# Delta rule: the 16x16 diagonal blocks inverted on VectorE, one block per partition, instead of in four doubling levels on TensorE

## The chip, the core and the metric

The kernel runs on one core of a Trainium2 chip. The metric is the device time of one execution in microseconds (us), lower being better. In the profile PE is TensorE (PEld its weight loads), DVE is VectorE, ACT is ScalarE, POOL is GpSimd and SP is SyncE, which issues the weight transfers.

## What is computed

Two decoder layers on 256 tokens of width 2048. Each has a mixer and a SwiGLU block, both with a residual and a layer norm. Layer 0's mixer is a gated short convolution beside a gated delta rule of 8 heads x 128; layer 1's is a sparse attention. The change is inside the delta rule:

```python
c = DN_CHUNK                                     # 64
a_mat = where(strict, einsum(kbeta, kc) * decay, 0.0)
rhs = concatenate([vc * bc, kbeta * exp(gc)[..., None]], axis=-1)
sol = triangular_solve(eye(c) + a_mat, rhs, left_side=True, lower=True, unit_diagonal=True)
...
v_new = u_i - w_i @ state
o     = q_i @ state + a_i @ v_new
state = state * gl + k_i.T @ v_new
```

The kernel solves the triangular system by building the inverse of (I + A). It works on chunks of 128 tokens, which gives the same result as the reference's chunks of 64.

## The kernel before

**Matmuls in three passes.** Every weight matrix comes in slabs of 1 MB. A slab is two *halves* of 128x1024. For each half ScalarE writes a rounded copy, `w_hi` (line 599), VectorE writes the rest, `w_lo` (line 1089), and TensorE runs three passes over the pair (lines 1792 to 1794), twelve matmuls of 512 columns. There are four slots for halves: ScalarE may write half h only when TensorE has used half h-4 (`half_used`), and VectorE follows ScalarE. In the program of each engine `halves(n)` (`z_halves(n)` on TensorE) stands where the next n halves are worked on. The order of everything is written out by hand; nothing moves at run time.

**The delta rule stage.** The 256 tokens are two tiles t, the 8 heads two groups hh of four; the four pairs (t, hh) are called *units*. All tiles of a unit are 128x512, four heads side by side. For every unit TensorE fills four PSUM banks (lines 2093 to 2102): `row` and `beta` are per-token numbers spread over all partitions (one matmul of `ones` with a tile that VectorE prepared, lines 1431 and 1432), `kk` and `kq` are products of keys and queries. VectorE makes AT (the transposed A) and the masked E from them (lines 1440 to 1453), with one Exp on ScalarE in between. `by_head` (line 2085) is four matmuls of 128x128, one for each head.

**The levels.** The inverse is built by doubling: given the inverse X of the diagonal blocks of width b (and its transpose T), one level gives that of width 2b. `BLOCKS` has seven levels. Level 0 takes no product: X = I - E on VectorE, then four transposes a unit on TensorE for T (`eT`, line 2105). Each of the levels 1 to 6 is, for each unit, `g` (E by T), a copy to SBUF by ScalarE (line 834), `x` (G by X) and, but for the last, `t` (X by G). VectorE subtracts the results and masks the next E (lines 1470 to 1472).

**Filler.** Between these steps TensorE works on the 16 halves of the next projection (z), `z_halves`: 1 before the units, 2 in each unit, 2 in the `eT` step, and 1 in each of the levels 1 to 5. ScalarE's `z_out` empties the z banks.

**After the stage.** The rest of the delta rule follows, then the output projection. SyncE loads x over the delta rule's tiles, so its queue waits for `gb_free` before it goes on (line 471); the weights behind it in the queue wait too.

Of the kernel before, what the change touches and what calls it, by code (L numbers as in the profile page):

```python
# [21 lines left out]
P = 128  # L22
# [30 lines left out]
BLOCKS = (1, 2, 4, 8, 16, 32, 64)  # L53
# [23 lines left out]
def trunk(nc, x_in, positions, ln_mix_g, ln_mix_b, ln_ffn_g, ln_ffn_b, ffn_w_in, ffn_w_out,  # L77
# [6 lines left out]
    with ctx:  # L84
# [33 lines left out]
        blk_mask = sb("blk_mask", [P, len(BLOCKS), P])  # L118
        lnT = sb("lnT", [P, 2, KT])
# [31 lines left out]
        def dn_tile(n):  # L151
            base, m = (gb_flat, n) if n < 8 else (vT_flat, n - 8)
            return base[:, m * 512:(m + 1) * 512].rearrange("p (h d) -> p h d", h=4)
        dn_more = sb("dn_more", [P, 12, 512], offset=x_at)

        def tiles_of(t, hh):

            if t == 0:
                return [dn_tile(6 * hh + n) for n in range(6)]
            return [dn_more[:, 6 * hh + n, :].rearrange("p (h d) -> p h d", h=4) for n in range(6)]  # L160
# [5 lines left out]
        norm_sq, norm_q = dn_tile(6), dn_tile(7)  # L166
# [78 lines left out]
        ident_ready, out_ready = sem("ident_ready"), sem("out_ready")  # L245
        for_act, for_pe, from_act, gb_free = sem("for_act"), sem("for_pe"), sem("from_act"), sem("gb_free")
# [22 lines left out]
        uses([("eT", t, hh) for t, hh in units])  # L269
# [111 lines left out]
        hands([("rows", t, hh) for t, hh in units])  # L381
        for n in range(len(BLOCKS)):
            hands([("m", t, n, hh) for t, hh in units])
# [120 lines left out]
        def _(pool):  # L504
# [22 lines left out]
            for n, b in enumerate(BLOCKS):  # L527

                v = blk_mask[:, n, :].rearrange("p (m a r) -> p m a r", a=2, r=b)[:, :, 1, :]
                own(pool.memset(v, 1.0))  # L530
                select(v, [[-2 * b, P // (2 * b)], [0, b]], 0, 1, 0.0)
                select(v, [[2 * b, P // (2 * b)], [0, b]], b - 1, -1, 0.0)
            pool.memset(eps_ln[:, :], LN_EPS).then_inc(consts, 1)
# [8 lines left out]
            def layer_norm(n, g, b):  # L542
                pool.wait_ge(gb_free, n + 1)
                if n:
                    pool.wait_ge(x_scaled, NT * n)
                for a, v in enumerate((g, b)):
                    pool.dma_start(gb[:, a, :], bcast(v, D)).then_inc(gb_in, 16)
                pool.dma_start(lnT[:, :, :], ln_by_feature[:, n, :, :]).then_inc(gb_in, 16)
            layer_norm(0, ln_mix_g[0], ln_mix_b[0])
# [36 lines left out]
        def _(act):  # L586
# [265 lines left out]
            for t, hh in units:  # L852
                wait_sp_read(act, ("row", t, hh))
                dt_ = tiles_of(t, hh)[0]
                done(act.activation(dt_, dt_, ACT.Exp))
                halves(2)
            halves(2)
            for n in range(1, len(BLOCKS)):
                for t, hh in units:
                    put(("g", t, n, hh), tiles_of(t, hh)[5])  # L860
                if n < len(BLOCKS) - 1:
                    halves(1)
                if n == 1:
                    z_out(0)
# [190 lines left out]
        def _(dv):  # L1055
# [248 lines left out]
            dv.wait_ge(consts, 3)  # L1304
            halves(LEAD)
# [98 lines left out]
            own(dv.scalar_tensor_tensor(nbe, egc, -1.0, beta, ALU.mult, ALU.mult))  # L1404
            for hh in range(2):
                wait_sp_read(dv, ("ktok", hh))
# [22 lines left out]
            for t, hh in units:  # L1429
                _, _, _, T, _, G = tiles_of(t, hh)  # L1430
                dv.tensor_tensor(G, bc(upper[:, :], 4), over(g_[:, heads_of(t, hh)], P), ALU.mult)
                to_pe(dv.tensor_tensor(T, bc(ident[:, :], 4), over(beta[:, heads_of(t, hh)], P), ALU.mult), ("rows", t, hh))
            halves(1)
            for t, hh in units:
                Dt, AT, E, T, X, G = tiles_of(t, hh)
                name = ("row", t, hh)
                wait_sp(dv, name)
                for h in range(4):
                    n = 8 * t + 4 * hh + h
                    ins = dv.scalar_tensor_tensor(Dt[:, h, :], sp4(name)[:, h, :], ngc[:, n:n + 1], neg_lower[:, :], ALU.add, ALU.add)  # L1440
# [12 lines left out]
                to_pe(dv.tensor_tensor(X, bc(ident[:, :], 4), E, ALU.subtract), ("m", t, 0, hh))  # L1453
                halves(2)

            for t, hh in units:
                Dt, AT, E, T, X, G = tiles_of(t, hh)
                name = ("eT", t, hh)
                wait_sp(dv, name)
                sp_out(dv.tensor_tensor(T, bc(ident[:, :], 4), sp4(name), ALU.subtract), name)  # L1460
                to_pe(dv.tensor_tensor(E, AT, bc(blk_mask[:, 1, :], 4), ALU.mult), ("m", t, 1, hh))
                if hh:
                    halves(1)
            for n in range(1, len(BLOCKS)):
# [12 lines left out]
                if n == 2:  # L1477
                    z_scaled(0)
# [291 lines left out]
        def _(pe):  # L1770
# [320 lines left out]
            def flat(tile):  # L2091
                return tile.rearrange("p h d -> p (h d)")
            for t, hh in units:
                v = slice(t * P, (t + 1) * P)
                _, _, _, T, _, G = tiles_of(t, hh)
# [12 lines left out]
            for n in range(1, len(BLOCKS)):  # L2108
                for t, hh in units:
                    _, _, E, T, X, G = tiles_of(t, hh)  # L2110
                    handed(("m", t, n, hh))
# [310 lines left out]
```

## Time and profile before

| | |
|---|---|
| time, median of 3 runs | 2503.22 us (2503.02 to 2504.13) |
| profiled execution, its own time | 2504.05 us |
| its span | 2502.3 us |
| PE busy | 2427.0 us, 97% |
| DVE busy | 1441.6 us, 58% |
| ACT busy | 1139.3 us, 46% |
| POOL busy | 30.2 us, 1% |
| HBM traffic | 175 GB/s over the span |
| mean granted clock of TensorE | 0.994 |

Busy times say how long an engine had work, not that it held the others up. The chain of waits follows the work that ended last back to its start. Matmul records overlap, so the pace of TensorE is read from the chain or from start to start, not from the mean of one record. An fp32 matmul shows as two records, an fp32 transpose or an fp32r matmul as one.

### The profile page before, as it was taken

To read this page: it belongs to the slowest core of one execution; us is meant where nothing else is said; L and a number is where in the kernel's file an instruction comes from. 1 tells how busy PE (TensorE), PEld (TensorE's weight loads), DVE (VectorE), ACT (ScalarE), POOL (GpSimd) and SP (SyncE) were. 2 spreads that over 40 slices of the span, in tenths; PEclk is the share of its full clock that TensorE was granted. 3 is DMA by queue.
4 is the path that set the end of the run, shared out by engine and by line. 5 is a ranking of instruction groups with operands and counts; after the bars stand their busy time and mean duration, and the time that the engine had idled before them with its cause. 6 is when DMAs were issued, how large, how long until landed. Compare 5 with 4: busy or idle time off the path is not lost.

```text
span 2502.3 us, 33337 instructions
## 1 busy us (share of the span) xinstructions
PE 2427.0 (97%) x12809; PEld 2079.1 (83%) x12809; DVE 1441.6 (58%) x1782; ACT 1139.3 (46%) x1527; POOL 30.2 (1%) x71
## 2 busy tenths in 40 slices
PE   8999999899999999999999998999999999999997
PEld 8999889777888888888879887888788888888886
DVE  5658676566444444455577756766644444445556
ACT  4445633444444444444454545554544444434443
POOL 2000000100000000000000000000000000000000
PEclk9999999999999999999999999999999999999999
DMA  7555431355555555555555653236555555555552
GB/s 254 185 168 185 152 101 51 152 186 168 190 196 177 193 188 196 203 201 197 189 185 159 231 186 101 85 101 219 164 179 195 186 196 188 184 200 214 191 195 107
DMA packets 179448, 437.99 MB, mean 175 GB/s; under 512 B 7104, under 2 KB 19504, under 8 KB 165280
## 3 DMA queue, kind: packets, MB, share of 16 engines
q1 hardware_dynamic: 177632, 427.85, 50.4%
q0 software_dynamic: 1728, 8.92, 0.9%
q8 instruction: 62, 1.02, 0.2%
q14 instruction: 26, 0.21, 0.0%
HBM read 434.64 MB, written 2.10 MB: 175 GB/s over the span
## 4 chain that ended last, share of the span: by engine, by line
PE 91%; DVE 5%; ACT 2%; DMA 1%; issue 1%; SPq 0%; DVEq 0%; ACTq 0%
PE bank L1792 28%; PE bank L1794 28%; PE bank L1793 28%; PE bank L2088 3%; PE bank L2321 1%; DVE w_lo L1089 1%; PE bank L2010 1%; PE bank L2294 1%; DMA raw<-in_hy_w_out_dram 1%; DVE stats L1164 1%; DVE x L1163 1%; DVE yt L1187 0%; ACT w_hi L599 0%; PE bank L2063 0%; PE bank L2312 0%
## 5 line engine op out<-in xcount | busy, mean ns | idle before, releaser
L1089 DVE TENSOR_TENSOR w_lo<-raw,w_hi 128x1024 fp32r<-128x1024 f32 x776 | 943.0, 1224 | 905.5 <-ACT w_hi L599 903.5
L599 ACT ACTIVATE w_hi<-raw 128x1024 fp32r<-128x1024 f32 x776 | 819.6, 1062 | 1072.7 <-PE bank L1794 1052.3
L1792 PE MATMUL bank<-w_hi,xt_hi 128*128 128x512 f32 x1904 | 750.0, 394 | 14.1 <-DVE w_lo L1089 8.3
L1794 PE MATMUL bank<-w_hi,xt_lo 128*128 128x512 f32 x1904 | 743.3, 390 | 0.0
L1793 PE MATMUL bank<-w_lo,xt_hi 128*128 128x512 f32 x1904 | 742.8, 390 | 0.0
L1792 PEld LDWEIGHTS bank<-w_hi,xt_hi 128*128 128x128 f32 x1904 | 358.8, 188 | 89.0 <-issue 10.0
L1794 PEld LDWEIGHTS bank<-w_hi,xt_lo 128*128 128x128 f32 x1904 | 358.5, 188 | 75.6
L1793 PEld LDWEIGHTS bank<-w_lo,xt_hi 128*128 128x128 f32 x1904 | 359.0, 189 | 72.5
L1792 PE MATMUL bank<-xt_hi,w_hi 128*128 128x256 f32 x928 | 267.7, 289 | 12.1 <-DVE w_lo L1089 12.1
L1792 PE MATMUL bank<-w_hi,a_hi 128*128 128x512 f32 x672 | 261.8, 390 | 2.0 <-ACT big L723 1.6
L1794 PE MATMUL bank<-xt_hi,w_lo 128*128 128x256 f32 x928 | 263.7, 284 | 0.0
L1793 PE MATMUL bank<-xt_lo,w_hi 128*128 128x256 f32 x928 | 263.7, 284 | 0.0
L1794 PE MATMUL bank<-w_hi,a_lo 128*128 128x512 f32 x672 | 261.5, 389 | 0.0
L1793 PE MATMUL bank<-w_lo,a_hi 128*128 128x512 f32 x672 | 261.4, 389 | 0.0
L1792 PEld LDWEIGHTS bank<-xt_hi,w_hi 128*128 128x128 f32 x928 | 179.3, 193 | 14.5 <-issue 11.6
L1793 PEld LDWEIGHTS bank<-xt_lo,w_hi 128*128 128x128 f32 x928 | 179.4, 193 | 2.0 <-issue 1.9
L1794 PEld LDWEIGHTS bank<-xt_hi,w_lo 128*128 128x128 f32 x928 | 179.3, 193 | 0.0
L1792 PEld LDWEIGHTS bank<-w_hi,a_hi 128*128 128x128 f32 x672 | 126.1, 188 | 29.4 <-issue 3.2
L1794 PEld LDWEIGHTS bank<-w_hi,a_lo 128*128 128x128 f32 x672 | 126.1, 188 | 26.3
L1793 PEld LDWEIGHTS bank<-w_lo,a_hi 128*128 128x128 f32 x672 | 126.2, 188 | 26.0
L1792 PE MATMUL bank<-spare_hi,xt_hi 128*128 128x512 f32 x80 | 33.1, 413 | 11.7 <-DVE spare_lo L1089 6.9
L714 ACT ACTIVATE yt<-bank 128x512 f32<-128x512 f32 x44 | 24.0, 597 | 43.5 <-PE bank L1794 43.5
(304 smaller groups left out, 1630.3 us busy)
## 6 DMA issues: line engine op xcount, KB each, us to landing
raw<-in_ffn_w_in_dram SPq DMA_DIRECT2D x176, 1024.0 KB, 5.1
raw<-in_ffn_w_out_dram SPq DMA_DIRECT2D x88, 1024.0 KB, 4.8
raw<-in_hy_w_in_dram SPq DMA_DIRECT2D x57, 1024.0 KB, 5.2
raw<-in_nsa_w_in_dram SPq DMA_DIRECT2D x41, 1024.0 KB, 5.1
raw<-in_hy_w_out_dram SPq DMA_DIRECT2D x16, 1024.0 KB, 5.0
raw<-in_nsa_w_out_dram SPq DMA_DIRECT2D x16, 1024.0 KB, 5.1
raw<-in_cmp_w_k_dram SPq DMA_DIRECT2D x4, 1024.0 KB, 6.4
raw<-in_cmp_w_v_dram SPq DMA_DIRECT2D x4, 1024.0 KB, 5.6
```

Of the source, the lines that this page charges most:

```text
L599: act.activation(weights_of(h)[0], half_of(h), ACT.Copy).then_inc(w_hi_ready, 1)
L714: ins = act.activation(sg[:, t, :], b[t][:, :], ACT.Silu)
L1089: dv.tensor_tensor(lo, half_of(h), hi.bitcast(F32), ALU.subtract).then_inc(w_lo_ready, 1)
L1163: own(dv.scalar_tensor_tensor(v, v, ALPHA, acc_bank(n, t, c)[:, :], ALU.mult, ALU.add))
L1164: ins = dv.bn_stats(stats[:, t, c, :], v)
L1792: pe.matmul(dst, l_hi, r_hi, start=start, stop=False, skip_group_check=shared)
L1793: pe.matmul(dst, l_hi, r_lo, start=False, stop=False, skip_group_check=shared)
L1794: return pe.matmul(dst, l_lo, r_hi, start=False, stop=stop, skip_group_check=shared)
L2010: ins = pe.transpose(b[:, f * SEQ + t * P:f * SEQ + (t + 1) * P], hid[:, t, (2 * a + f) * P:(2 * a + f + 1) * P], ident[:, :])
L2088: ins = pe.matmul(b[:, h * P:(h + 1) * P], lhs(h), rhs(h), start=True, stop=True)
L2294: ins = pe.matmul(b[:, h * kn:(h + 1) * kn], qT[:, 4 * g + hp * k + h, v], ksT[:, br, g, 0:kn], start=True, stop=True)
L2321: ins = pe.matmul(b[:, h * P:(h + 1) * P], pT_buf[br][:, k, h * P:(h + 1) * P], vs[:, br, k, g * DH:(g + 1) * DH], start=k == 0, stop=k == t)
```

## The change

A new buffer layout puts each kind of tile of all 16 (tile, head) pairs side by side: `AT_all`, `T_all`, `X_all` and so on. The levels 1, 2, 4 and 8 of `BLOCKS` go, with their masks. In their place VectorE inverts all 128 diagonal 16x16 blocks at once, one block on each partition. Four transposes of 32 partitions x 512 bring the blocks over. For 14 columns j, each a multiply and an add that need the result of the one before, the elimination runs along the free dimension. Eight more transposes write the result into T and X, which GpSimd has set to zero. In the diff the part at line 546 is GpSimd's, that at 853 ScalarE's, those at 1426 and 1450 VectorE's, and that at 2090 TensorE's. `low_half` tells which of the two blocks of a 32x32 square a partition has. TensorE's `row` and `beta` become four matmuls each of a broadcast column with `ident`, so VectorE prepares no tiles for them. The filler z halves are handed out anew: 1, then 1 in each unit, 9 behind the last unit, and 1 in each of the first two levels left.

```diff
-BLOCKS = (1, 2, 4, 8, 16, 32, 64)
+BASE = 16
+BLOCKS = (16, 32, 64)
...
+        dn_more = sb("dn_more", [P, 3, 2048], offset=x_at)
+        def all_heads(v):
+            return v.rearrange("p (m d) -> p m d", m=16)
+        AT_all, T_all = all_heads(gb_flat[:, 0:2048]), all_heads(gb_flat[:, 2048:4096])
+        X_all, Dt_all, E_all, G_all = all_heads(vT_flat), *(all_heads(dn_more[:, n, :]) for n in range(3))
...
+        base_rows = base_flat[:, 0:512].rearrange("p (c r) -> p c r", c=BASE)
+        base_wide = base_flat[:, 512:1024].rearrange("p (i s j) -> p i s j", i=BASE, s=2)
@@ -546,6 +567,12 @@
+            pool.memset(T_all, 0.0).then_inc(base_cleared, 1)
+            wait_sp(pool, ("vtok", NT - 1, 1))
+            pool.memset(X_all, 0.0).then_inc(base_cleared, 1)
@@ -853,15 +880,15 @@
                 done(act.activation(dt_, dt_, ACT.Exp))
-                halves(2)
-            halves(2)
-            for n in range(1, len(BLOCKS)):
+                halves(1)
+            halves(6)
+            z_out(0)
+            halves(3)
+            for n in range(len(BLOCKS)):
@@ -1426,10 +1456,6 @@
-            for t, hh in units:
-                _, _, _, T, _, G = tiles_of(t, hh)
-                dv.tensor_tensor(G, bc(upper[:, :], 4), over(g_[:, heads_of(t, hh)], P), ALU.mult)
-                to_pe(dv.tensor_tensor(T, bc(ident[:, :], 4), over(beta[:, heads_of(t, hh)], P), ALU.mult), ("rows", t, hh))
@@ -1450,18 +1476,43 @@
                 own(dv.tensor_tensor(E, AT, bc(blk_mask[:, 0, :], 4), ALU.mult))
-                to_pe(dv.tensor_tensor(X, bc(ident[:, :], 4), E, ALU.subtract), ("m", t, 0, hh))
-                halves(2)
-
-            for t, hh in units:
-                Dt, AT, E, T, X, G = tiles_of(t, hh)
-                name = ("eT", t, hh)
-                wait_sp(dv, name)
-                sp_out(dv.tensor_tensor(T, bc(ident[:, :], 4), sp4(name), ALU.subtract), name)
-                to_pe(dv.tensor_tensor(E, AT, bc(blk_mask[:, 1, :], 4), ALU.mult), ("m", t, 1, hh))
-                if hh:
-                    halves(1)
-            for n in range(1, len(BLOCKS)):
+                halves(1)
...
+            for rows, cols in quadrants():
+                ins = dv.transpose(base_rows[rows], AT_all[rows, :, cols].rearrange("p m (s c) -> p c s m", s=2))
+            own(ins)
+            halves(1)
+            low, high = low_half[:, 4:5], low_half[:, 5:6]
+            own(dv.scalar_tensor_tensor(base_neg, base_rows[:, :, 0:BASE], low, base_rows[:, :, BASE:], ALU.mult, ALU.add))
+            own(dv.tensor_tensor(base_neg, base_neg, base_below[:, :, :], ALU.mult))
+            own(dv.tensor_tensor(base_inv, base_neg, base_ident[:, :, :], ALU.add))
+            halves(1)
+            for j in range(1, BASE - 1):
+                n = BASE - 1 - j
+                step = base_step[:, 0:n, 0:j]
+                own(dv.tensor_tensor(step, base_neg[:, j + 1:, j:j + 1].to_broadcast([P, n, j]),
+                                     base_inv[:, j:j + 1, 0:j].to_broadcast([P, n, j]), ALU.mult))
+                own(dv.tensor_tensor(base_inv[:, j + 1:, 0:j], base_inv[:, j + 1:, 0:j], step, ALU.add))
+                if j % 4 == 0:
+                    halves(1)
+            halves(1)
+            dv.tensor_scalar(base_wide[:, :, 0, :], base_inv, low, None, ALU.mult)
+            own(dv.tensor_scalar(base_wide[:, :, 1, :], base_inv, high, None, ALU.mult))
+            dv.wait_ge(base_cleared, 2)
+            for rows, cols in quadrants():
+                dv.transpose(T_all[rows, :, cols].rearrange("p m (s j) -> p j s m", s=2), base_wide[rows].rearrange("p i s j -> p j s i"))
+            halves(2)
+            for rows, cols in quadrants():
+                ins = dv.transpose(X_all[rows, :, cols].rearrange("p m (s i) -> p i s m", s=2), base_wide[rows])
+            to_pe(ins, ("base",))
+            halves(1)
+            for n in range(len(BLOCKS)):
@@ -2090,25 +2141,22 @@
-                handed(("rows", t, hh))
-                for name, m in (("row", G), ("beta", T)):
-                    b = sp_use((name, t, hh))
-                    sp_done(pe.matmul(b[:, :], ones[:, :], flat(m), start=True, stop=True), (name, t, hh))
+                m = 8 * t + 4 * hh
+                for name, row in (("row", 4), ("beta", 2)):
+                    by_head((name, t, hh), lambda h: sm[:, row, m + h:m + h + 1].to_broadcast([P, P]), lambda h: ident[:, :])
...
-                z_halves(2)
-            for t, hh in units:
-                handed(("m", t, 0, hh))
-                transposes(("eT", t, hh), [tiles_of(t, hh)[2][:, h, :] for h in range(4)])
-                if hh:
-                    z_halves(1)
-            for n in range(1, len(BLOCKS)):
+                z_halves(1)
+            z_halves(9)
+            handed(("base",))
+            for n in range(len(BLOCKS)):
```

**The order on VectorE**, from the last unit to the first level on TensorE. Before (names: `w_lo` is a half; `gb`, `big` and `dn_more` hold the units' tiles; `bank` is PSUM):

```order
L1452 TENSOR_TENSOR dn_more<-dn_more,blk_mask 128x512
L1453 TENSOR_TENSOR dn_more<-ident,dn_more 128x512
L1089 TENSOR_TENSOR w_lo<-raw,w_hi 128x1024 x2
L1460 TENSOR_TENSOR gb<-ident,bank 128x512
L1461 TENSOR_TENSOR gb<-gb,blk_mask 128x512
L1460 TENSOR_TENSOR big<-ident,bank 128x512
L1461 TENSOR_TENSOR big<-gb,blk_mask 128x512
L1089 TENSOR_TENSOR w_lo<-raw,w_hi 128x1024
L1460 TENSOR_TENSOR dn_more<-ident,bank 128x512
```

and now:

```order
L1116 TENSOR_TENSOR w_lo<-raw,w_hi 128x1024
L1488 STREAM_TRANSPOSE dn_more<-gb 32x512 x4
L1116 TENSOR_TENSOR w_lo<-raw,w_hi 128x1024
L1492 SCALAR_TENSOR_TENSOR dn_more<-dn_more,low_half 128x256
L1493 TENSOR_TENSOR dn_more<-dn_more,base_below 128x256
L1494 TENSOR_TENSOR dn_more<-dn_more,base_ident 128x256
L1116 TENSOR_TENSOR w_lo<-raw,w_hi 128x1024
L1499 TENSOR_TENSOR dn_more<-dn_more 128x14
L1501 TENSOR_TENSOR dn_more<-dn_more 128x14
...
L1509 STREAM_TRANSPOSE gb<-dn_more 32x16x2x16 x4
L1116 TENSOR_TENSOR w_lo<-raw,w_hi 128x1024 x2
L1512 STREAM_TRANSPOSE big<-dn_more 32x16x2x16 x4
```

The product for `eT` and the subtract before it are gone. The transposes, the three operations on 128x256 and the chain of small operations stand in their place, with halves between them.

**The order on TensorE** in the same place, before, with the z halves' rows left out:

```order
L2099 MATMUL bank<-dn_more,ones 128x512 x2
L2088 MATMUL bank<-big 128x128 x8
...
L2063 MATMUL bank<-ident,gb 128x128 x4
L2063 MATMUL bank<-ident,big 128x128 x4
...
L2063 MATMUL bank<-ident,dn_more 128x128 x8
...
L2088 MATMUL bank<-gb 128x128 x4
L2088 MATMUL bank<-big 128x128 x4
L2088 MATMUL bank<-dn_more 128x128 x8
```

and now:

```order
L2139 MATMUL bank<-ident,sm 128x128 x8
L2139 MATMUL bank<-big 128x128 x8
...
L2139 MATMUL bank<-gb,dn_more 128x128 x16
...
L2139 MATMUL bank<-big,dn_more 128x128 x4
L2139 MATMUL bank<-dn_more,big 128x128 x4
```

The matmuls with `ones` became twice four with `ident`. Where `eT` and the first of the levels stood there are now only halves (ten of them, the unit's one and the nine), and behind them the `g` of the first level left, which waits for VectorE's last transpose.

## Rows read from the trace of the kernel before

**Rows 1.** The page: engines' busy time, and the chain by engine.
```profile
PE 2427.0 (97%) x12809; PEld 2079.1 (83%) x12809; DVE 1441.6 (58%) x1782; ACT 1139.3 (46%) x1527; POOL 30.2 (1%) x71
...
PE 91%; DVE 5%; ACT 2%; DMA 1%; issue 1%; SPq 0%; DVEq 0%; ACTq 0%
```

**Rows 2.** Windows: stretch, length, busy PE, PEld, DVE, ACT, POOL, clock, DMA, GB/s.
```profile
380.00:390.00 10.00, 10.00 (x89) 9.87 (x88) 9.37 (x15) 2.34 (x4) 0.00 (x0) 1.00 0.01 2
```

**Rows 3.** Chain of waits, delta rule stage: start, length in us, what.
```profile
324.72 1.72 PE bank L2099 x4
...
351.71 0.87 PE bank L2063 x8
...
365.25 10.72 PE bank L2088 x96
...
378.70 10.72 PE bank L2088 x96
```

**Rows 4.** Waits, stage: who waited for whom, us in total, times, longest.
```profile
ACT w_hi L599 <- PE bank L1794: 38.2, 19, 3.3
...
PE bank L2099 <- DVE gb L1432: 0.4, 1, 0.4
```

**Rows 5.** Timeline of DVE, the first unit: start, length, what.
```profile
320.08 1.12 DVE L1440 SCALAR_TENSOR_TENSOR gb<-bank,sm,neg_lower 128x128 f32<-128x128 f32 x4
...
324.55 0.69 DVE L1453 TENSOR_TENSOR gb<-ident,gb 128x512 f32<-128x512 f32 x1
325.16 2.35 DVE L1089 TENSOR_TENSOR w_lo<-raw,w_hi 128x1024 fp32r<-128x1024 f32 x2
```

**Rows 6.** Timeline of DVE, two chained small operations.
```profile
307.01 0.17 DVE L1398 COPY sm<-bank 128x16 f32<-128x16 f32 x1
307.22 0.17 DVE L1399 TENSOR_SCALAR sm<-sm 128x16 f32<-128x16 f32 x1
```

**Rows 7.** DVE by line and shape: count | busy us, mean ns | idle before.
```profile
L1350 DVE RECIPROCAL gb<-gb 128x512 f32<-128x512 f32 x8 | 26.8, 3347 | 0.0
...
L1584 DVE TENSOR_TENSOR yt<-big 128x240 f32<-128x240 f32 x16 | 8.0, 583 | 2.0 <-ACT big L941 2.0
...
L1637 DVE TENSOR_TENSOR yt<-yt 128x256 f32<-128x256 f32 x12 | 5.0, 420 | 0.0
...
L1314 DVE TENSOR_SCALAR big<-gb,misc_w 128x256 f32 x16 | 4.6, 349 | 8.0 <-ACT gb L761 8.0
...
L1692 DVE TENSOR_TENSOR big<-big 128x60 f32<-128x60 f32 x8 | 1.7, 216 | 0.3
...
L1699 DVE TENSOR_TENSOR sm<-sm 128x12 f32<-128x12 f32 x8 | 1.4, 172 | 0.3
```

**Rows 8.** Chain behind the stage, where TensorE starts again after a pause.
```profile
491.93 1.07 ACT w_hi L599
493.02 1.24 DVE w_lo L1089
494.39 0.77 PE bank L1792
495.16 0.43 PE bank L1793
...
498.04 0.23 PE bank L1794
```

**Rows 9.** Windows in that pause and behind it.
```profile
486.00:488.00 2.00, 0.70 (x4) 0.24 (x2) 0.00 (x0) 0.00 (x0) 0.00 (x0) 1.00 1.01 411
488.00:490.00 2.00, 0.00 (x0) 0.00 (x0) 0.00 (x0) 0.00 (x0) 0.00 (x0) 1.00 0.64 223
...
494.00:496.00 2.00, 1.61 (x4) 1.35 (x5) 2.00 (x5) 1.90 (x5) 0.00 (x0) 0.50 1.02 426
```

**Rows 10.** Waits of SyncE's queue, 440 to 500 us.
```profile
SPq L473 <- DVE sm L1074: 44.8, 1, 44.8
```

**Rows 11.** Timeline of POOL: a memset of 128x896.
```profile
2.27 0.84 POOL L524 MEMSET blk_mask<- 128x896 f32 x1
```

More of the change, by code:

```diff
@@ L118, in trunk @@
         blk_mask = sb("blk_mask", [P, len(BLOCKS), P])
+        base_ident = sb("base_ident", [P, BASE, BASE])
+        base_below = sb("base_below", [P, BASE, BASE])
+        low_half = sb("low_half", [P, 6])
         lnT = sb("lnT", [P, 2, KT])
@@ L149, in trunk @@
         gb_flat = gb[:, :, :].rearrange("p a n -> p (a n)")
[L151 to L154, printed above, removed]
-        def tiles_of(t, hh):
-            if t == 0:
-                return [dn_tile(6 * hh + n) for n in range(6)]
-            return [dn_more[:, 6 * hh + n, :].rearrange("p (h d) -> p h d", h=4) for n in range(6)]
+        dn_more = sb("dn_more", [P, 3, 2048], offset=x_at)
[3 more added lines that the diff above has]
+        X_all, Dt_all, E_all, G_all = all_heads(vT_flat), *(all_heads(dn_more[:, n, :]) for n in range(3))
+        def tiles_of(t, hh):
+            m = 8 * t + 4 * hh
+            return [v[:, m:m + 4, :] for v in (Dt_all, AT_all, E_all, T_all, X_all, G_all)]
+        base_flat = dn_more[:, 2, :]
+        base_rows = base_flat[:, 0:512].rearrange("p (c r) -> p c r", c=BASE)
+        base_wide = base_flat[:, 512:1024].rearrange("p (i s j) -> p i s j", i=BASE, s=2)
+        base_neg = base_flat[:, 1024:1280].rearrange("p (i j) -> p i j", i=BASE)
+        base_inv = base_flat[:, 1280:1536].rearrange("p (i j) -> p i j", i=BASE)
+        base_step = base_flat[:, 1536:1792].rearrange("p (i j) -> p i j", i=BASE)
         units = [(t, hh) for t in range(NT) for hh in range(2)]
@@ L165, in trunk @@
         ba_out = yt[:, KT - 1, :]
-        norm_sq, norm_q = dn_tile(6), dn_tile(7)
+        norm_sq, norm_q = (gb_flat[:, n:n + 512].rearrange("p (h d) -> p h d", h=4) for n in (3072, 3584))
         hT = big[:, 0:FT * SEQ].rearrange("p (f t) -> p f t", f=FT)
@@ L380, in trunk @@
         hands([("g",)])
-        hands([("rows", t, hh) for t, hh in units])
-        for n in range(len(BLOCKS)):
+        hands([("rows",), ("base",)])
+        for n in range(1, len(BLOCKS)):
             hands([("m", t, n, hh) for t, hh in units])
@@ L532, in _ @@
                 select(v, [[2 * b, P // (2 * b)], [0, b]], b - 1, -1, 0.0)
+            own(pool.memset(base_ident[:, :, :], 0.0))
+            own(pool.affine_select(out=base_ident[:, :, :], in_=base_ident[:, :, :], pattern=[[1, BASE], [-1, BASE]], compare_op=ALU.not_equal,
+                                   fill=1.0, base=0, channel_multiplier=0))
+            own(pool.memset(base_below[:, :, :], -1.0))
+            select(base_below[:, :, :], [[1, BASE], [-1, BASE]], -1, 0, 0.0)
+            own(pool.memset(low_half[:, 0:4], 1.0))
+            select(low_half[:, 0:4], [[-2 * BASE, 4]], 0, 1, 0.0)
+            select(low_half[:, 0:4], [[2 * BASE, 4]], BASE - 1, -1, 0.0)
             pool.memset(eps_ln[:, :], LN_EPS).then_inc(consts, 1)
@@ L862, in _ @@
                     halves(1)
-                if n == 1:
-                    z_out(0)
             z_out(1)
@@ L1304, in _ @@
             dv.wait_ge(consts, 3)
+            own(dv.tensor_reduce(low_half[:, 4:5], low_half[:, 0:4], AX.X, ALU.add))
+            own(dv.tensor_scalar(low_half[:, 5:6], low_half[:, 4:5], -1.0, 1.0, ALU.mult, ALU.add))
             halves(LEAD)
@@ L1404, in _ @@
             own(dv.scalar_tensor_tensor(nbe, egc, -1.0, beta, ALU.mult, ALU.mult))
+            to_pe(mark(), ("rows",))
             for hh in range(2):
@@ L1464, in _, with quadrants @@
-            for n in range(1, len(BLOCKS)):
+                halves(1)
+            def quadrants():
+                for q in range(P // 32):
+                    rows = slice(32 * q, 32 * q + 32)
+                    yield rows, rows
+            for rows, cols in quadrants():
[3 more added lines that the diff above has]
+            low, high = low_half[:, 4:5], low_half[:, 5:6]
@@ L1476, in _ @@
                     halves(1)
-                if n == 2:
+                if n == 1:
                     z_scaled(0)
@@ L2092, in flat @@
                 return tile.rearrange("p h d -> p (h d)")
+            handed(("rows",))
             for t, hh in units:
                 v = slice(t * P, (t + 1) * P)
[L2095 to L2099 removed]
+                m = 8 * t + 4 * hh
+                for name, row in (("row", 4), ("beta", 2)):
+                    by_head((name, t, hh), lambda h: sm[:, row, m + h:m + h + 1].to_broadcast([P, P]), lambda h: ident[:, :])
                 by_head(("kk", t, hh), lambda h: qkvT[:, 8 + 4 * hh + h, v], lambda h: qkvT[:, 8 + 4 * hh + h, v])
                 by_head(("kq", t, hh), lambda h: qkvT[:, 8 + 4 * hh + h, v], lambda h: qkvT[:, 4 * hh + h, v])
[L2102 to L2108 removed]
+                z_halves(1)
+            z_halves(9)
+            handed(("base",))
+            for n in range(len(BLOCKS)):
                 for t, hh in units:
                     _, _, E, T, X, G = tiles_of(t, hh)
[L2111 removed]
+                    if n:
+                        handed(("m", t, n, hh))
                     by_head(("g", t, n, hh), lambda h: E[:, h, :], lambda h: T[:, h, :])
```

4 lines of the change are left out of this document (3 added, 1 removed).

## The prediction

> **What bounds the kernel now.** I read the page first: TensorE is busy 97% of the span, and 91% of the chain of waits is TensorE's own work [rows 1]. So what TensorE no longer does is won one for one, provided that it always has something else to do. Then I read the stage that changes, the delta rule between 314 and 434 us. In a stretch taken from its middle TensorE is busy 10.00 of 10.00 us with the clock at full speed, VectorE 9.37 of 10.00 [rows 2], and the chain runs through TensorE's small fp32 products without a gap [rows 3]. Two things follow. First, the levels are on the path. Second, VectorE is near its limit in places, and it is VectorE that gets the new work. The question is therefore whether the nine z halves that are now put behind the last unit last as long as VectorE's inversion. If they don't, TensorE stands still for the first time in this stage.
>
> **What TensorE loses.** In the chain `x` and `t` of one level and `g` of the next are one piece of 96 records in 10.72 us, 0.112 us a record [rows 3]. Three such sets go (widths 2, 4, 8; a set is 48 products, two records each): 3 x 10.72 = 32.2 us. The `eT` transposes go: two pieces of 0.87 us [rows 3] = 1.7 us. The `row` and `beta` products change form: four records of 128x512 took 1.72 us a unit [rows 3]; now they are 16 records of 128x128, 16 x 0.112 = 1.79 us, so 4 x 0.07 = 0.3 us more. That a broadcast column as weights costs the same as a full tile isn't in the trace. Below, it can't beat 0 by much, since the records are already paced like all others; above, if it took twice the pace, 4 x 1.79 = 7 us more. I take 0, since nothing in the pace of the other products depends on what they read. The wait of `row` for VectorE's prepared tiles goes, 0.4 us [rows 4], because the only condition left is met before the value transposes end. The 16 z halves stay, all of them. Sum: 32.2 + 1.7 - 0.3 + 0.4 = 34.0 us, if nothing waits.
>
> **What VectorE gets.** I follow it from the end of the last unit's z half on TensorE, since everything is in lockstep from there: ScalarE's `w_hi` waits for TensorE's halves, 38.2 us in 19 waits [rows 4], starts as soon as one is used, and VectorE's `w_lo` follows.
>
> - In the unit loop VectorE needs 324.55 - 320.08 = 4.5 us from its first operation to the one that is removed [rows 5], and a half (two last 2.35 us with an overlap of 0.08, so 1.14 us each from start to start). TensorE needs 32 x 0.112 = 3.6 us and one half. A half on TensorE is 378.70 - 365.25 - 10.72 = 2.7 us [rows 3], so a unit takes 6.3 us. VectorE, which begins each unit 2.3 us behind TensorE's half (1.07 for ScalarE, 1.24 for its own part [rows 8]), still empties the banks in time. The loop stays TensorE's.
> - The base begins 2.3 us after the last unit's half. Its parts: eight halves before the last transpose, 8 x 1.18 = 9.4 us (0.04 for the wait on the operation before). Three operations of 128x256, 0.42 each and 0.04 for the wait [rows 7] = 1.4 us. 28 chained small ones: 0.21 us from start to start with 16 elements [rows 6], and (216 - 172)/(60 - 12) = 0.9 ns for each element more [rows 7]. They have 1120 elements in all, 672 above 16 each: 28 x 0.207 + 0.6 = 6.4 us. Two that widen the result, 0.35 each [rows 7] = 0.7 us. Together 17.9 us.
> - Twelve transposes of 32 partitions x 512, T each. No row shows one. From below, T is 0.60: a dense operation of 512 elements lasts 0.69 and the next starts 0.61 after it (324.55 to 325.16 [rows 5]). From above, the slowest operation with 512 elements is the reciprocal, 3.35 us [rows 7]. Between them the nearest row is L1584: it is the one that reads with a long stride (16 words between neighbours), and it takes 583 ns for 240 elements where a dense one takes 420 for 256 [rows 7]. At 0.9 to 1.0 ns an element the dense one of 240 would be 0.40, so the stride costs 0.18/240 = 0.75 ns an element. All twelve transposes read or write with strides of 32 to 128 words. For 512 elements: 0.69 + 0.38 = 1.07 us. I take T = 1.07.
>
> The rule that speaks against this change is one of layout. On L1584 the stride of 64 bytes cost 0.18 us [rows 7]. The Trainium skill (SBUF — State Buffer, "Door 1: The DMA port swizzle") has it that memory is read in lines of 16 bytes and that each access which goes to a new line pays. By that rule every element of a strided transpose pays, as in L1584; without it the T above would be 0.69. The trace agrees as far as reads go, and shows no strided write.
>
> There is a second one. VectorE's operations on all 128 partitions start 0.61 apart though each lasts 0.69 [rows 5]. The Trainium skill (VectorE: DVE Perf Modes, "Two Vector instructions with no wait between them") says that an instruction which starts in another group of 32 partitions than the one before is held until that has finished. The four transposes of a set do just that. By the rule the overlap of 0.08 is lost twelve times, 1.0 us in all; no run here shows it yet.
>
> **The balance.** VectorE hands the base over 2.3 + 17.9 + 12T = 20.2 + 12T after the last unit's half, TensorE has 9 x 2.73 = 24.6 us of halves. The wait is 12T - 4.4: at T = 1.07 that is 8.4 us. At 0.69 it is 3.9, at 0.60 it is 2.8. The halves on VectorE are not late in this: the last that TensorE needs is ready some 3 us before its turn even at T = 1.07. The last of the eight waits for ScalarE, behind TensorE's eighth of the nine halves; that is 2.3 us of TensorE's time before the nine end, and VectorE is later than that by itself.
>
> After a pause TensorE pays once more. Behind the stage it stood from about 486.7 (0.70 us of work in the 2 us from 486, none from 488 to 490) to 494.4 [rows 8, 9], and in the stretch where it starts again the granted clock is 0.50, that is 1.2 GHz instead of 2.4. The chain gives 0.43 us for a matmul there and 0.23 from 498.04 on [rows 8]. From 494.39 to 498.04 it did eight, 3.65 us instead of 8 x 0.23 = 1.84, of which some 0.2 is the start. I charge 1.6 us for one pause of 8 us. For one of 3 us it could be 0 or 1.6.
>
> Other edits I cost at nothing. GpSimd's two memsets of 128x2048 are at most 2048/896 x 0.84 = 1.9 us each [rows 11] and are due 30 us later. The two small operations of `low_half` stand at the start, where VectorE waits for `w_hi`. ScalarE's `z_out(0)` comes earlier, in time it has. The level 64 now has `z_scaled(0)`, 1.4 us on VectorE, ahead of its subtractions, which fills a gap of about that length. SyncE's queue waits 44.8 us for VectorE at the end of the stage [rows 10], so the burst of x and weights behind it moves with the stage and its own pause stays as long as it is.
>
> Sum: 34.0 - 8.4 - 1.6 = 24.0 us less. Against the profiled execution's own time, 2504.05 us (span 2502.3), that is 2480.0; on the median of the runs, 2503.2, it is 2479.2.
>
> **The rivals.**
>
> *The cover holds.* If the transposes were as cheap as the cheapest rows and the chained operations a little cheaper than 0.21, TensorE would wait under 2 us and keep its clock: 34 - 2 = 32 less, 2471. For it: TensorE's z halves are 24.6 us long, and the sum without the transposes is 20.2. Against it: 12T is then at most 6.4, T = 0.53, under the pace of any row with 512 elements.
>
> *The transposes are slow.* Strided reads and writes might both pay, or a 4-byte transpose might need more than one pass. With T = 2.0, about halfway between 1.07 and the reciprocal's 3.35, the wait is 19.6 and 34.0 - 19.6 - 1.6 = 12.8 is left: 2490. For it: nothing in the trace bounds a transpose well, and eight of the twelve write with a stride. Against: the only strided row costs half as much again, not three times.
>
> *VectorE becomes the bound of the stage.* The same place, the other side: at T = 3.35 the wait is 35.8, and 34.0 - 35.8 - 1.6 = -3.4, so 2506.6, slower. It turns at T = 36.8/12 = 3.07 us. For it: an operation of that pace exists. Against: that one does a division, a transpose only moves.
>
> *The gain is given back behind the stage.* If the output projection's weights came at times of their own, TensorE would only wait longer for them: 2503. For it: its pause at 486 to 494 is a wait for transfers, and nine halves in a row draw 4.5 slabs in 24.6 us, 190 GB/s. Against: the queue waits for VectorE's mark [rows 10], and in the stage the slabs' readers wait for TensorE, not for transfers [rows 4].
>
> **How the numbers follow.** The forecast, T from 0.6 to 1.5 and one pause: 66%, with 2472 to 2485 as its own range. The cover holds: 7%. Slow transposes, T from 1.5 to 2.7: 17%. VectorE the bound: 4%. Given back: 3%. The change doing something else than it says, such as the broadcast weights at half pace, is in the second half of the range: 3%. The predicted time is 2479. The range that should hold it 8 times in 10 goes from 2471.5 to 2489. A measurement of this kernel can tell about 0.2% from no change, 5 us, that is 2498 to 2508. Faster by more: 92%; within: 4%; slower: 4%.
>
> **What would show it.** On TensorE behind the last unit: nine z halves without a gap, then one wait for VectorE's last transpose, of 8 us if I am right, 3 to 4 if T is 0.7; a clock of 0.50 for some 3 us behind it. On VectorE: twelve transposes of about 1.07 us, 28 small operations 0.2 to 0.25 apart. The levels left at 13.45 us apiece with their half, as before. `row` and `beta` at 0.112 us a record. The pause in front of the output projection as long as before. I would be wrong if the transposes lie outside 0.6 to 1.5, if a z half in the nine waits for `w_lo`, or if the pause behind the stage grows.

## The result and the profile after

The changed kernel takes 2483.88 us (median of 4 runs, 2483.34 to 2485.32) where the one before took 2503.59 beside it (4 runs, 2503.02 to 2504.13). The ratio is 0.9922 [0.9910, 0.9934]: 19.7 us less, where 24 were forecast. Between the two profiled executions it is 2504.05 - 2483.76 = 20.3 us. The time lies in the stated range, at the slower end of the forecast's own (2472 to 2485). Some 4 us of the expected gain are missing, and most of them have an address.

The page of the changed kernel, to be read against [rows 1]:

```profile
span 2481.8 us, 32769 instructions
...
PE 2394.5 (96%) x12553; PEld 2050.7 (83%) x12553; DVE 1429.8 (58%) x1774; ACT 1130.0 (46%) x1515; POOL 27.4 (1%) x68
...
PE 89%; DVE 6%; ACT 2%; DMA 1%; issue 1%; SPq 0%; DVEq 0%; ACTq 0%
```

TensorE does 32.5 us less, near the 33.6 of work that was worked out (34.0 without the 0.4 of a wait). But its share of the chain went down by two points and VectorE's went up by one: now VectorE is on the path somewhere. VectorE's busy time has even gone down, by 11.8 us. That says nothing about the path, since the new work lies where TensorE waits for it.

The chain of waits through the stage (start, length in us, what):

```profile
307.43 1.79 DVE sm L1428
...
318.45 3.57 PE bank L2139 x32
324.79 3.57 PE bank L2139 x32
...
343.87 1.07 ACT w_hi L626
345.03 1.23 DVE w_lo L1116
346.26 1.02 DVE dn_more L1488
...
376.35 1.05 DVE big L1512
377.45 6.12 PE bank L2139 x32
386.31 10.72 PE bank L2139 x96
399.76 14.30 PE bank L2139 x128
...
456.12 16.39 DMA raw<-in_hy_w_out_dram
```

The 16 products of a unit (`row`, `beta`, `kk` and `kq`, two records each) are one piece of 32 records in 3.57 us, 0.112 us a record, and a unit begins 6.33 us after the one before it. From the last unit's half on (343.9) the chain leaves TensorE and goes through ScalarE and VectorE until 377.4: 33.6 us, where 33.0 had been worked out. Then `g` of the first level left takes 6.12 us for 32 records, which in the units took 3.57.

The waits in the stage (engine, line, who was waited for: us in total, times, longest):

```profile
PE bank L2139 <- DVE big L1512: 9.2, 1, 9.2
...
PE bank L2114 <- ACT big L861: 2.9, 1, 2.9
```

TensorE waits 9.2 us for the last of VectorE's transposes, where 8.4 were forecast, and no z half in the nine waits for its `w_lo`; the wait of 0.4 us [rows 4] is gone. VectorE's timeline in that stretch (start, length, what):

```profile
346.17 4.44 DVE L1488 STREAM_TRANSPOSE dn_more<-gb 32x512 f32<-32x512 f32 x4
...
351.79 0.48 DVE L1492 SCALAR_TENSOR_TENSOR dn_more<-dn_more,low_half 128x256 f32<-128x256 f32 x1
...
354.37 0.18 DVE L1499 TENSOR_TENSOR dn_more<-dn_more 128x14 f32<-128x14 f32 x1
354.58 0.18 DVE L1501 TENSOR_TENSOR dn_more<-dn_more 128x14 f32<-128x14 f32 x1
...
366.18 4.78 DVE L1509 STREAM_TRANSPOSE gb<-dn_more 32x512 f32<-32x512 f32 x4
370.97 2.36 DVE L1116 TENSOR_TENSOR w_lo<-raw,w_hi 128x1024 fp32r<-128x1024 f32 x2
373.25 4.14 DVE L1512 STREAM_TRANSPOSE big<-dn_more 32x512 f32<-32x512 f32 x4
```

Counted from each set's start to the start of what follows it, the twelve transposes take 4.48 + 4.79 + 4.17 = 13.44 us, 1.12 each where 1.07 was taken. The three operations of 128x256 take 1.44 us (1.4), and the 28 chained ones, in four groups with halves between, 6.57 (6.4). And the windows around the wait (columns as in [rows 2]):

```profile
372.00:376.00 4.00, 0.00 (x0) 0.00 (x0) 3.97 (x5) 0.00 (x0) 0.00 (x0) 0.50 0.61 210
376.00:380.00 4.00, 2.55 (x12) 2.56 (x13) 2.60 (x3) 0.44 (x1) 0.00 (x0) 0.50 0.19 62
```

TensorE stands still, and when it starts the granted clock is 0.50 (1.2 GHz instead of 2.4). In slices of 1 us it is 0.50 until 382 and 1.00 from 383 on, so it is low for some 4.7 of the 6.12 us. `g` costs 6.12 - 3.57 = 2.55 us more, where 1.6 was charged.

The longer wait (0.8) and this (0.95) account for 1.75 us. The rest is lost in front of the stage, where the change does nothing on TensorE. VectorE's timeline there:

```profile
307.23 0.17 DVE L1427 COPY sm<-bank 128x16 f32<-128x16 f32 x1
307.43 1.78 DVE L1428 TENSOR_SCALAR sm<-sm 128x16 f32<-128x16 f32 x1
309.24 0.17 DVE L1429 TENSOR_TENSOR sm<-bank,sm 128x8 f32<-128x8 f32 x1
...
313.51 1.23 DVE L1438 TENSOR_TENSOR big<-big,sm 128x1024 f32<-128x1024 f32 x1 [1.69 <-ACT big L861]
314.77 1.23 DVE L1116 TENSOR_TENSOR w_lo<-raw,w_hi 128x1024 fp32r<-128x1024 f32 x1
```

and GpSimd's:

```profile
307.38 1.81 POOL L573 MEMSET gb<- 128x2048 f32 x1 [294.06 <-DVE yt L1419]
314.18 1.80 POOL L575 MEMSET big<- 128x2048 f32 x1 [5.00 <-PE bank L2114]
```

L1428 is the operation of 0.17 us in [rows 6] (L1399 there). It now takes 1.78, and it ends 0.02 us after the new memset on GpSimd. The second memset lies beside two operations with two inputs from SBUF, and they take what they always take. Behind the stall, the granted clock from 310 to 320 is 0.83. Before:

```profile
310.00:320.00 10.00, 8.42 (x44) 6.39 (x45) 8.24 (x11) 5.89 (x9) 0.00 (x0) 1.00 0.32 105
```

after:

```profile
310.00:320.00 10.00, 7.15 (x38) 6.05 (x37) 2.95 (x5) 6.78 (x11) 1.80 (x1) 0.83 0.28 96
```

Of the twelve z matmuls between 314.12 and 318.45 the first eight run at 0.43 us each, the pace of 1.2 GHz in [rows 8], and the last four at 0.23: 8 x 0.20 = 1.6 us. So the stage's first unit begins at 318.45 instead of 315.47, 3 us late: 0.2 that is there before the memset (VectorE's `yt` begins at 306.03 against 305.81), 1.6 of the stall and 1.6 of the clock, less the 0.4 that `row` no longer waits. The rest of it is won as planned: the output projection's first transfer (the last row of the chain above) came at 475.47 before, 19.35 us later, and is as long as it was (16.39 against 16.44 us).

### The profile page after: what moved, and what is told of

Same layout as the page of the kernel before. It is cut to its first block, busy times and chain, and to the rows that moved or that the text cites. A ratio compares the mean times of both kernels' runs of the same rounds, so it can differ in the third digit from the quotient of the medians.

```text
span 2481.8 us, 32769 instructions
## 1 busy us (share of the span) xinstructions
PE 2394.5 (96%) x12553; PEld 2050.7 (83%) x12553; DVE 1429.8 (58%) x1774; ACT 1130.0 (46%) x1515; POOL 27.4 (1%) x68
## 4 chain that ended last, share of the span: by engine, by line
PE 89%; DVE 6%; ACT 2%; DMA 1%; issue 1%; SPq 0%; DVEq 0%; ACTq 0%
PE bank L1843 28%; PE bank L1845 28%; PE bank L1844 28%; PE bank L2139 2%; DVE w_lo L1116 1%; PE bank L2369 1%; PE bank L2061 1%; PE bank L2342 1%; DMA raw<-in_hy_w_out_dram 1%; DVE stats L1191 1%; ACT w_hi L626 1%; DVE x L1190 1%; DVE yt L1214 0%; PE bank L2114 0%; PE bank L2360 0%
```

## Experiments

Four questions were open. What holds the 16-element operation for 1.8 us (the memset beside it: A1 in e2, by the form of the operation, or A2, whatever the form; or B in e1, another cause, such as the layout)? Does the slow clock in front of the stage come from that stall (in the expectations A, it does; C, it would have come anyway)? Are the transposes slow by their strides, and are they held one behind the other? How much of the base's wait is the length of the chain, and how much the halves between? Times are medians; the kernel before took 2503.05 to 2503.3 beside them.

**e1: the memset later.** GpSimd waits for VectorE's mark `rows` (all the small operations are done by then) before the first memset, so that it lies beside no operation with one input. Only the wait is new; the memset is shown to place it.

```diff
+            pool.wait_ge(for_pe, FP[("rows",)])
             pool.memset(T_all, 0.0).then_inc(base_cleared, 1)
```

> The changed kernel, but GpSimd's first memset waits until VectorE has handed over `rows`, so that it runs beside no tensor_scalar. In the changed kernel that memset ran from 307.38 to 309.19 us and VectorE's tensor_scalar on 128x16 (ngc) from 307.43 to 309.21, 1.78 us where it took 0.17 before; TensorE's pause behind it was longer, and the clock fell to 1.2 GHz for the first z half. Theory A (the memset holds up the tensor_scalar, and the longer pause costs the clock): ngc takes 0.17 us again, the first unit on TensorE starts at 315.3 instead of 318.45, the clock stays at 1.00 between 310 and 320, and the whole is 3.2 us faster than the changed kernel, about 2480.7. Theory B (the long tensor_scalar had another cause, such as the new buffer layout or where the memory lies): ngc stays at 1.8 us, and the time at 2483.9. Theory C (the memset holds it up, but the clock would have fallen anyway): 1.6 us faster, 2482.3, with a clock of 0.83 in 310 to 320.

Measured: 2480.72 us (2479.02 to 2483.98, 4 runs), ratio 0.9911 [0.9895, 0.9928]. VectorE and GpSimd in front of the stage:

```profile
307.48 0.17 DVE L1429 TENSOR_SCALAR sm<-sm 128x16 f32<-128x16 f32 x1
```

```profile
310.40 1.80 POOL L574 MEMSET gb<- 128x2048 f32 x1 [298.33 <-DVE sm L1102]
```

The stall is gone, and with it 1.6 us of the chain: its small operations follow each other as before. In the times it is 2.1 us less than the changed kernel (e8, below), though the runs of the two overlap. The clock from 310 to 320 is 0.83 all the same:

```profile
310.00:320.00 10.00, 8.58 (x53) 7.98 (x54) 4.83 (x9) 6.25 (x9) 3.61 (x2) 0.83 0.33 105
```

The median is the one that theory A gave (2480.7), but the trace is theory C's: the first unit begins at 316.54, where A had 315.3, and the clock is down. The four runs lie 5 us apart, which is more than the step from A to C, so the time decides nothing here. The stall is shown to be the memset's. The fall of the clock isn't: it came without the stall.

**e2: the same value by another operation.** `ngc` is made with two inputs from SBUF instead of one; the memset stays where it is.

```diff
-            own(dv.tensor_scalar(ngc, gc_, -1.0, None, ALU.mult))
+            own(dv.scalar_tensor_tensor(ngc, gc_, -2.0, gc_, ALU.mult, ALU.add))
```

> The changed kernel with the memset where it was; the one tensor_scalar beside it (ngc = -gc) is now a scalar_tensor_tensor with the same result. Theory A1 (it is the form of the operation that decides: a tensor_scalar in fp32 from SBUF, which runs at two elements a cycle, waits for GpSimd, one with two tensors does not): it takes 0.18 us although the memset runs at the same time, and the first unit starts at 315.3. Theory A2 (any VectorE operation that starts beside the memset waits for it): it takes 1.8 us as before, first unit at 318.4.

Measured: 2482.86 us (one run). VectorE's timeline:

```profile
306.55 0.17 DVE L1428 SCALAR_TENSOR_TENSOR sm<-sm 128x16 f32<-128x16 f32 x1
306.76 0.17 DVE L1429 TENSOR_TENSOR sm<-bank,sm 128x8 f32<-128x8 f32 x1
306.96 1.37 DVE L1431 COPY sm<-sm 128x8 f32<-128x8 f32 x1
```

The memset ran from 306.49 to 308.30. The operation with two inputs inside that time takes 0.17 us, the next one (one input from PSUM, one from SBUF) too, and then a copy of eight elements, its one input from SBUF, is held until 308.33. So the form decides, not the size and not the data. Little was won, 1.78 - 1.37 = 0.41 us on the chain, since the wait only moved to the next operation of the wrong form, and ScalarE needs that one as well.

The Trainium skill (SBUF — State Buffer, "Who interferes with whom") says of this that VectorE and GpSimd share one pair of ports, which whoever came first holds for the whole instruction; copies and `tensor_scalar` can go into the mode that needs the pair, and an operation with two inputs from SBUF is in the way only of a GpSimd instruction that reads SBUF, which a memset doesn't. The trace agrees in each case: 1.78 and 1.37 us for one input from SBUF, 0.17 and 1.23 for two.

**e7: only the memset, in the kernel before.** The same memset of 128x2048 with the same condition in front of it is put into the kernel before, with nothing else of the change.

```diff
+            pool.memset(gb_flat[:, 2048:4096], 0.0).then_inc(base_cleared, 1)
...
+            dv.wait_ge(base_cleared, 1)
```

> The kernel before, with one thing added: GpSimd's memset of 128x2048 in the place where the changed kernel has it. Theory A (the memset by itself holds up ngc): ngc takes 1.8 us instead of 0.17, the first product of the first unit (315.47 before) starts 1.6 us later, or 3 with a fall of the clock, and the time is 2504.6 to 2506. Theory B (it takes the changed layout too): ngc 0.17 us, 2503.

Measured: 2503.97 us (one run), within what can be told from no change; the time alone decides nothing. The trace does:

```profile
306.86 1.78 DVE L1403 TENSOR_SCALAR sm<-sm 128x16 f32<-128x16 f32 x1
```

Its operation is held as in the changed kernel and the clock from 310 to 320 is 0.83. The last piece of the stage's chain comes at 421.19 instead of 419.06, though the operations in front of the memset came 0.36 us earlier (305.45 against 305.81): 2.5 us in the stage. In the span this is not seen (2502.2). The chain is still 2.4 us late at 1627 us, in layer 1, and 0.8 late at 1675. Between the two lies the clock. There TensorE waits twice for ScalarE, 1.2 and 0.7 us, in both kernels. In the kernel before the clock falls behind the waits, with nine matmuls at 0.33 to 0.43 us; here it doesn't, and they take 0.23. Before, then here (2 us later, where the same work lies):

```profile
1630.00:1640.00 10.00, 8.89 (x39) 7.24 (x39) 7.50 (x13) 4.27 (x10) 0.00 (x0) 0.83 0.34 107
```

```profile
1632.00:1642.00 10.00, 8.48 (x49) 7.25 (x50) 8.17 (x16) 4.68 (x11) 0.00 (x0) 1.00 0.34 111
```

The edit adds nothing near this place. So the same instructions behind the same waits can cost 1.6 us of clock in one profile and nothing in another.

**e3: dense transposes.** All three sets read and write contiguous runs of 512 elements (the first of the three edits is shown). The kernel then moves other numbers than the solve needs, so this is about time alone.

```diff
-                ins = dv.transpose(base_rows[rows], AT_all[rows, :, cols].rearrange("p m (s c) -> p c s m", s=2))
+                ins = dv.transpose(base_flat[rows, 0:512], gb_flat[rows, 0:512])
...
```

> The changed kernel with the twelve transposes over contiguous 32x512 stretches, read and written without a stride; they move other numbers than the solve needs, the rest is as it was. In the changed kernel a transpose takes 1.12 us (reads with a stride), 1.20 (both) and 1.04 (writes with a stride). Theory A (the strides cost what they cost in L1584): 0.69 us each, or 0.61 from start to start if a change of the partition group does not hold the next one; the base is handed over 5 us earlier and TensorE waits 4 us instead of 9.2. Theory B (a 4-byte transpose takes two cycles an element whatever the layout): 1.05 to 1.2 us each, the wait stays at about 9.

Measured: 2479.69 us (one run). VectorE by line and shape (count | busy us, mean ns | idle before), first of the changed kernel:

```profile
L1509 DVE STREAM_TRANSPOSE gb<-dn_more 32x512 f32<-32x512 f32 x4 | 4.7, 1185 | 0.1
L1488 DVE STREAM_TRANSPOSE dn_more<-gb 32x512 f32<-32x512 f32 x4 | 4.4, 1100 | 0.0
L1512 DVE STREAM_TRANSPOSE big<-dn_more 32x512 f32<-32x512 f32 x4 | 4.1, 1026 | 0.0
```

and dense:

```profile
L1509 DVE STREAM_TRANSPOSE gb<-dn_more 32x512 f32<-32x512 f32 x4 | 2.8, 703 | 0.1
L1512 DVE STREAM_TRANSPOSE big<-dn_more 32x512 f32<-32x512 f32 x4 | 2.8, 702 | 0.0
L1488 DVE STREAM_TRANSPOSE dn_more<-gb 32x512 f32<-32x512 f32 x4 | 2.8, 701 | 0.0
```

The strides cost 0.40 us where only the read has one (L1488), 0.33 where only the write has (L1512), and 0.49 where both have (L1509). The prediction's 0.38, taken from the one strided row in [rows 7], was near all three, also near the write, which it had no row for. Four dense ones take 2.8 us = 4 x 0.70, while operations on all partitions that last 0.69 start 0.61 apart [rows 5]: each starts only when the one before it has finished, which is what the second rule in the prediction says. The first of a set starts in the same group of partitions as the half before it, and it does overlap: in the changed kernel the two halves end at 370.97 + 2.36 = 373.33 and the set begins at 373.25. That speaks for the change of group. No run has two transposes in one group, so whether a transpose holds its successor by itself is not shown.

The base's wait went from 9.2 to 4.4 us. The `g` behind it took even longer, 6.69 us. So a pause half as long cost no less of TensorE's clock.

**e4: three halves behind the base.** VectorE's order is changed so that three of the z halves between its steps come after the last transpose. The chain of the base is the same work.

```diff
-            halves(1)
...
-            halves(2)
...
-            halves(1)
+            halves(4)
```

> The changed kernel, but three of VectorE's halves that stand before the last transpose (one before the widening, two between the sets of transposes) stand behind it; TensorE needs them only after it has the base. Theory A (VectorE's chain sets the end of the wait): the base comes 3.4 us earlier, TensorE waits 5.8 us instead of 9.2, the clock cost of that pause stays, and the time is 3.4 us below the changed kernel, about 2480.5. Theory B (ScalarE or a transfer sets it, or the halves are missed at once behind the base): no change, 2483.9, with a wait for `w_lo` in front of the z half behind the first `g`.

Measured: 2479.05 us (2477.96 to 2481.15), ratio 0.9904 [0.9888, 0.9921]. The wait:

```profile
PE bank L2137 <- DVE big L1510: 5.8, 1, 5.8
```

3 x 1.15 = 3.4 us less, as counted. Here too `g` took 6.02 us.

**e5: the second of the two results handed over later.** The level's `g` needs `T` alone; `X` is first read behind `g`. The base is handed over after the transposes of `T`, and `X` with a mark of its own. One half stands between the two sets and three come behind both; the widened result lies in another free buffer.

```diff
-        hands([("rows",), ("base",)])
+        hands([("rows",), ("base",), ("base_x",)])
...
+            to_pe(ins, ("base_x",))
+            halves(3)
...
+                if n == 0:
+                    handed(("base_x",))
```

> The changed kernel, but the base is handed over as soon as T is written, and X by itself four transposes later: `g` needs only E and T, and X is due 6.3 us later (a `g` of 3.57 and a half of 2.73). Three halves of VectorE stand behind all of it, one between the two sets of transposes; the widened result lies in another free buffer, since ScalarE's copy of `g` goes over the old one. Theory A (the wait is VectorE's chain, and a third of the transposes need not be in it): the wait of 9.2 us shrinks by 2 x 1.14 + 1.14 for the halves and by 4.2 for the transposes, to about 1.6. If the clock falls only after a longer pause than that, its 1.9 to 3.1 us go too: 2473; if it falls all the same, 2476. Theory B (the wait moves to X: a pause in front of the first `x`): little better than with the halves behind alone, 2479.

Measured: 2472.26 us (one run). The waits, and the chain:

```profile
PE bank L2139 <- DVE gb L1508: 1.7, 1, 1.7
```

```profile
368.51 3.84 PE bank L2139 x32
...
375.12 10.79 PE bank L2139 x96
```

The wait is 1.7 us and `g` takes 3.84: the clock stays at full speed (1.00 in the windows from 360 to 390).

**e6: e5 and e1 together**, with no other edit.

> The one before with GpSimd's first memset later as well. Theory A: the two act in different places and add up, 1.6 to 1.9 us below the one before, 2471 to 2475, which is below the changed kernel (2483.9) and each of the single steps (2480.7 and 2479.1). Theory B (what is won in front of the stage only makes TensorE wait longer at the base): as the one before.

Measured: 2470.23 us (2469.45 to 2471.84, 4 runs), ratio to the kernel before 0.9866 [0.9851, 0.9881], just under the 2471 to 2475 expected. The wait is 1.7 and `g` 3.84 again. Its windows:

```profile
310.00:320.00 10.00, 9.53 (x62) 8.59 (x63) 6.08 (x10) 5.83 (x9) 3.07 (x2) 1.00 0.32 105
...
370.00:380.00 10.00, 10.00 (x81) 9.59 (x80) 9.96 (x14) 1.40 (x2) 0.00 (x0) 1.00 0.57 207
```

The clock is 1.00 in front of the stage too, for the first time with the change in. This version beats the kernel before by 33 us and the changed one by 12.6.

**e8: the changed kernel once more**, beside the others, to have its time and its pauses a second time.

> The changed kernel once more, on the same chip as the ones before, to compare them with: 2483.9. If the clock behind the pauses depends on chance, the first `g` (6.12 us before) and the first z half (4.33) vary between 3.6 and 6.7 and between 2.8 and 4.6 from run to run.

Measured: 2482.84 us (2482.1 to 2483.57, 5 runs), ratio 0.9917 [0.9903, 0.9930]. The held operation takes 1.78 us again, the wait is 9.2 again, `g` 5.73. The 12.6 us between it and e6 come out of their parts: 7.5 of the base's wait, 5.73 - 3.84 = 1.9 of `g`, and 3.3 of the stage's first unit, which begins at 314.36 instead of 317.64: 12.7. Of the 3.3, 1.6 are the stall and 1.6 the clock.

## Why the prediction was right, and where it was not

The direction, the mechanism and the place of the new wait were right. By its own terms:

- **What TensorE loses, 34.0.** Right, and 0.26 short: the first `row` of the kernel before, behind its wait, took 1.98 us where the others took 1.72. The three sets and `eT` are gone, `row` and `beta` go at 0.112 us a record, so broadcast weights cost nothing more, and the other levels keep their 10.72 us [rows 3].
- **The transposes, T = 1.07.** 1.12, which is 0.6 us over twelve. e3 shows that the stride costs 0.33 to 0.49 us of each, on the write side as well, and that the transposes of a set don't overlap. The rule cited there (the Trainium skill, SBUF — State Buffer, "Door 1: The DMA port swizzle"), that each access to a new line pays, agrees: without strides they take 0.70.
- **The base's chain, 33.0 us.** 33.6. With nine halves that ended at 377.45 - 9.20 = 368.25, where 343.87 + 24.6 = 368.4 was counted, the wait is 9.2, against 8.4: 0.8 us lost.
- **One pause's clock cost, 1.6.** 2.55 here, and 1.9 to 3.1 over the runs with such a wait. It was sized by eight large matmuls at half speed [rows 8, 9], 3.65 us long. Here the clock was low for 4.7 us. Some 0.27 of the 2.55 isn't clock but the start after a wait (`g` took 3.84 in e5 and e6, at full clock); the prediction had taken 0.2 for it out of its own row and then left it out of the sum. Another 0.95 us.
- **The step that failed: the memsets "at most 1.9 us each" and costed at nothing, since they "are due 30 us later".** The size was right. What was asked was when their result is needed, and not what lies beside them. A memset holds a VectorE operation with one input for as long as it runs, and the one it met is among the chained small ones that ScalarE, then TensorE wait for: 1.6 us (e1, e2, e7).
- **The rest in front of the stage** is the clock of the z matmuls, another 1.6 us. The prediction left it out. e1 shows that it comes without the stall.

24.0 - 0.8 - 0.95 - 1.6 - 1.6 = 19.05; with 0.26 for the first `row` and 0.2 for the later arrival it is 19.1, against 19.35 read off the chain behind the stage, and 19.7 between the medians. That the time fell inside the forecast's own range is owed to its width: the four larger misses all cost time.

Of the rivals, slow transposes and the bound on VectorE fell (T = 1.12). Nothing was given back behind the stage: the transfers moved with it. The rival in which the cover holds fell as a forecast, but e5 shows that it was within reach, with the same transposes: by what is handed over first and by where the halves stand. Its price was right too: a wait under 2 us with the clock kept, and 2472 and 2470 us for its 2471.

**What stays open** is what decides whether the clock falls. Ahead of the eight value transposes in front of the stage TensorE stands for 2.75 to 2.85 us in nine of the ten profiles, and for 4.0 in e2. Behind that the clock fell in the changed kernel, e1 to e5, e7 and e8, and not in the kernel before and e6. e1 and e6 have the same order there and the same pause (2.76 and 2.75). So neither the memset nor the order decides it. What e7's profile shows in layer 1 is the same: equal instructions and equal waits, and the clock fell once and once not. The runs of one kernel point that way too: the four of e1 have a mean clock of 0.990 to 0.993, and the two at 0.993 are the two fastest (2479.02 and 2479.65, the others 2481.78 and 2483.98). So the 1.6 us in front of the stage can't be counted as a cost of the change, nor their absence as a gain of e6: of the 12.6 us by which e6 beats e8, 1.6 hang on this.

## What to carry to other kernels

When work goes from a busy engine to another, the gain is what the busy one no longer does, minus the part of the other's chain that its cover doesn't reach, counted from the chain's last input to its last handover. So put only that work in the chain which the next step needs, hand over what is read first by itself, and let the filler work come behind. Charge a wait for TensorE's clock as well: in this kernel all six waits of 4.4 to 9.2 us cost 1.9 to 3.1 us more than themselves, and the two of 1.7 us cost 0.27 more. Even short waits aren't safe, since 1.2 and 0.7 us in a row cost 1.6 in one profile and nothing in another. And an instruction on an idle engine isn't free because nobody is in a hurry for it: look at what runs beside it, above all a GpSimd memset beside VectorE copies and `tensor_scalar` operations from SBUF.

## What the runs showed of the hardware

- A `tensor_scalar` of 128x16 took 1.78 us instead of 0.17 and a copy of 128x8 took 1.37, each beside a memset of 128x2048 on GpSimd (1.81), while operations of 128x16 and 128x1024 with two SBUF inputs kept their 0.17 and 1.23 us.
- A VectorE transpose of 32x512 in fp32 takes 0.70 us dense, 1.03 with a strided write, 1.10 with a strided read, 1.19 with both; four on the four groups of partitions don't overlap (4 x 0.70 = 2.8 us).
- After a wait of 4.4 to 9.2 us, 32 small fp32 records took 5.47 to 6.69 us instead of 3.57, and the length of the wait didn't order them (6.69 was behind 4.4). After 1.7 us they took 3.84, in two profiles.
- Behind pauses of 2.75 to 2.85 us TensorE's clock fell in seven of nine profiles. Behind waits of 1.2 and 0.7 us in layer 1 it was 0.83 over 10 us in the kernel before and 1.00 in e7.
- A TensorE product of 128x128 in fp32 whose weights are a broadcast column takes 0.112 us a record, two records each, the same as one with a full tile.
